# Another order of the on-chip buffers in a three-part transformer block

## The reference

```python
def _swiglu(x, w_in, w_out):
    a, b = jnp.split(x @ w_in, 2, axis=-1)
    return (jax.nn.silu(a) * b) @ w_out

for layer in range(DEPTH):
    h = h + 0.5 * _swiglu(_rmsnorm(h, ffn1_norm[layer]), ffn1_w_in[layer], ffn1_w_out[layer])
    ...
    h = h + 0.5 * _swiglu(_rmsnorm(h, ffn2_norm[layer]), ffn2_w_in[layer], ffn2_w_out[layer])
```

## Time and profile before

| what | value |
|---|---|
| time of the profiled run | 2951.99 us |
| its span, first to last instruction | 2950.2 us |
| median of three runs | 2957.29 us |
| TensorE matmul busy | 2768.1 us, 94% |
| GpSimd busy | 1653.9 us, 56% |
| VectorE busy | 1369.8 us, 46% |
| ScalarE busy | 694.1 us, 24% |
| q1, the queue of the kernel's own DMAs | 234.21 MB, 25.7% of 16 DMA engines |
| mean granted clock of TensorE | 0.972 |

### The profile page before, as it was taken

One profiled execution on the slowest core, in us unless ns is written; L12 is line 12 of the kernel. 1 busy time (PEld: TensorE's weight loads), 2 busy tenths in 40 slices (PEclk: granted clock), 3 DMA queues, 4 the chain that ended last, 5 costly groups with the idle time before them and its releaser, 6 DMA issues. The chain is left out here.

```text
span 2950.2 us, 36065 instructions
## 1 busy us (share of the span) xinstructions
PE 2768.1 (94%) x13132; PEld 2200.9 (75%) x13132; DVE 1369.8 (46%) x1623; ACT 694.1 (24%) x1168; POOL 1653.9 (56%) x966
## 2 busy tenths in 40 slices
PE   7999989766799999997899999999999999999999
PEld 5777768543678888875688888878888866788887
DVE  8878842145453143115654143754144466543142
ACT  3444320233210011026421011121011166321010
POOL 4666746300456566650266566666666678666565
PEclk9999999877899999999999999999999989999999
DMA  4222223100223232320133232333233200133232
GB/s 168 93 93 97 88 79 91 52 0 0 72 79 114 78 103 89 96 83 1 35 94 110 82 100 94 100 120 107 86 99 96 71 7 2 37 99 114 78 96 89
DMA packets 62023, 235.59 MB, mean 80 GB/s; under 512 B 6880, under 2 KB 7008, under 8 KB 61792
## 3 DMA queue, kind: packets, MB, share of 16 engines
q1 hardware_dynamic: 61920, 234.21, 25.7%
HBM read 232.08 MB, written 2.10 MB: 79 GB/s over the span
## 5 line engine op out<-in xcount | busy, mean ns | idle before, releaser
L314 POOL TENSOR_TENSOR w_lo<-ring,w_hi 128x1024 fp32r<-128x1024 f32 (+2 forms) x396 | 1026.7, 2593 | 57.8 <-issue 2.6
L312 POOL CAST w_hi<-ring 128x1024 fp32r<-128x1024 f32 (+2 forms) x396 | 454.0, 1146 | 1040.2 <-PE ps L332 801.5
L330 PE MATMUL ps<-hi,w_hi 128*128 128x512 f32 x2064 | 811.4, 393 | 12.4 <-DVE lo L1381 4.6
L332 PE MATMUL ps<-hi,w_lo 128*128 128x512 f32 x2064 | 805.4, 390 | 0.0
L331 PE MATMUL ps<-lo,w_hi 128*128 128x512 f32 x2064 | 805.3, 390 | 0.0
L330 PEld LDWEIGHTS ps<-hi,w_hi 128*128 128x128 f32 x2064 | 388.7, 188 | 99.6 <-DVE lo L1381 6.5
L331 PEld LDWEIGHTS ps<-lo,w_hi 128*128 128x128 f32 x2064 | 388.6, 188 | 82.3 <-issue 2.6
L332 PEld LDWEIGHTS ps<-hi,w_lo 128*128 128x128 f32 x2064 | 388.6, 188 | 81.8
L330 PE MATMUL ps<-hid_hi,w_hi 128*128 128x512 f32 x704 | 274.4, 390 | 0.0
L331 PE MATMUL ps<-hid_lo,w_hi 128*128 128x512 f32 x704 | 274.0, 389 | 0.0
L332 PE MATMUL ps<-hid_hi,w_lo 128*128 128x512 f32 x704 | 273.9, 389 | 0.0
(11 more groups left out here) (307 smaller groups left out, 3441.4 us busy)
## 6 DMA issues: line engine op xcount, KB each, us to landing
ring<-in_ffn_in SPq DMA_DIRECT2D x176, 512.0 KB, 3.6
ring<-in_even_in SPq DMA_DIRECT2D x48, 512.0 KB, 4.4
ring<-in_ffn_out SPq DMA_DIRECT2D x32, 768.0 KB, 4.2
ring<-in_ffn_out SPq DMA_DIRECT2D x32, 640.0 KB, 3.8
ring<-in_even_out SPq DMA_DIRECT2D x16, 512.0 KB, 3.6
ring<-in_odd_v SPq DMA_DIRECT2D x8, 512.0 KB, 3.6
ring<-in_odd_qk SPq DMA_DIRECT2D x8, 512.0 KB, 3.6
ring<-in_odd_r SPq DMA_DIRECT2D x8, 512.0 KB, 3.6
```

Source lines behind the costliest of these rows:

```text
L312: nc.gpsimd.tensor_copy(w_hi[:, j % 2, 0:cols], ring[:, j, 0:cols])
L314: nc.gpsimd.tensor_tensor(w_lo[:, j % 2, 0:cols], ring[:, j, 0:cols], w_hi[:, j % 2, 0:cols].bitcast(F32), ALU.subtract).then_inc(sem["w_r ...
L330: nc.tensor.matmul(bank, w_hi[:, j % 2, w], x_hi[:, k, :], start=(start and k == 0), stop=False)
L332: mm = nc.tensor.matmul(bank, w_lo[:, j % 2, w], x_hi[:, k, :], start=False, stop=(stop and k == kt - 1))
```

## The change

The ten pieces of SBUF are laid down in another order. Sizes, names, instructions and their order on each queue stay as they are.

```diff
-        for name, cols in (("consts", (N_CONSTS + 7) // 8 * 8), ("small", 16), ("masks", 2 * P), ("res", DT * T),
-                           ("hi", DT * T), ("ring", RING * SLOT), ("root", T), ("rinv", T), ("acc", T), ("arena", ARENA)):
+        for name, cols in (("res", DT * T), ("hi", DT * T), ("ring", RING * SLOT), ("consts", (N_CONSTS + 7) // 8 * 8),
+                           ("root", T), ("rinv", T), ("acc", T), ("small", 16), ("masks", 2 * P), ("arena", ARENA)):
             put(name, cols)
```

## The result

The changed kernel takes 2991.33 us, the median of four runs (2990.14 to 3000.12), against 2956.15 us for four runs of the kernel before (2951.99 to 2961.56). The ratio is 1.0121, with a 95% interval of 1.0106 to 1.0138. The prediction was 2955 us, with a range of 2945 to 2968; both missed it. The profiled run took 2993.0 us, with a span of 2991.2 us.

A forecast was written before the change was run, and what follows sets the result against it. The prediction took TensorE, busy 94% of the span, as the bound. All terms were 0, so 2951.99 us for the profiled run plus 0; toward the three-run median of 2957.29 it said 2955 us, range 2945 to 2968.

The forecast's parts named there:

- Distance costs nothing: 0 us for the 8,304 matmuls of these two operand sets.: TensorE matmuls streaming `hi` or `hid_hi`: how far apart operands lie does not matter, since both showed 226.7 ns; 0 us.
- The 64-byte remainder: TensorE matmuls streaming `hi`, whose start goes from remainder 32 to 0 by 64 bytes: 0 us, bounded by 58 either way.
- +58 us: Upper bound on TensorE's loss if remainder 32 was the good case: 13.4 ns for each of 4,320 `hi` matmuls.
- the −58 side: Rival, faster through TensorE: `hi` at a multiple of 64 loses its excess per column, giving 2894 us; chance 0.05.
- the slower side: Outcome more than 0.3% slower, chance 0.09: through GpSimd's slots (0.06) or through TensorE's granted clock (0.03).
- VectorE: Durations at L1407, L245 and L1622 do not depend on start addresses: 0 us, at most 1 us at L245.
- GpSimd: Cast and subtraction per `ring` slot, covered by 1.86 us of idle time: 0 us, bounded by 6.5 us either way.
- the rival: GpSimd's subtraction slows from unlike remainders of `ring` and `w_hi`: 2965 us at 20% more per slot; chance 0.06.
- DMA: Landings before the first matmul at 10.80 us and first-layer weights: 0 us, at most 1.1 us at the start.
- the rival through the clock: Shifted VectorE and GpSimd phases move dips of TensorE's clock; two more 10 us stretches give 2962 us; chance 0.03.
- a rule on addresses "that all operands of before met by chance": Closing sign that the prediction is wrong: some engine has such a rule; no size or chance given.

The follow-up runs named there:

- run 2: Kernel before with `hi` 32 bytes further and what follows it 64 (distance 224 between `hi` and `w_hi`, mod 256): 2997.38 us.
- run 3: Kernel before with all pieces moved 32 bytes further: 2954.61 us.
- run 5: Kernel before with only the split weights `w_hi` and `w_lo` 32 bytes further, no stream moved: 3023.65 us, beside 2952.89 for the kernel before.
- run 6: Kernel before with `hi` 64 bytes further and what follows 128, `res` staying (distance 192 from `hi` to `w_hi`, mod 256): 3008.13 us.
- run 4: Kernel before with `res` and `ring` put at multiples of 64 and `hi` at remainder 32 by 64 (distance 192 to `w_hi`, mod 256): 3006.18 us.
- run 7: Kernel before with `ring` and all behind it, weights included, 128 bytes further and `hi` staying (distance 128): 2974.66 us.
- run 10: Separate kernel, TensorE alone on zeros: matmul triples at 16 stream-to-weights distances, both streams or one moved, plus float32 and bfloat16 matmuls; 338.9 us in all.
- run 9: Changed kernel with `arena` 32 bytes further, so `hi` to weights is a multiple of 256: 2953.03 us against 2961.07 for the kernel before, ratio 0.998.
- run 8: Kernel before with `ring` alone 32 bytes further, the rest moved by 256 or 0: 2956.18 us.
- run 1: Changed kernel with `res` to `ring` 32 bytes further and what follows 64 (distance 0): 2957.21 us, beside 2951.69 for the kernel before.
- run 11: Separate kernel, TensorE alone, zeros as output: one stream at several distances to the weights, then pairs with streams and weights moved one by one; 183.23 us in all.

## Why the prediction was wrong

**"Distance costs nothing: 0 us for the 8,304 matmuls of these two operand sets."** This is the step that failed. The earlier trace rows do show `hi` and `hid_hi` 77 KB apart at the same 226.7 ns. But both are multiples of 256 bytes from the weights, so the rows compared one case with itself, and the 0 was carried over to a case that they did not hold. What counts is the distance to the weights that are read beside the stream, by its remainder mod 256 (runs 2, 3, 5, 6). The table of the change had the fact: `hi` moves by 27,872 bytes, 108 x 256 + 224, and `arena`, with the weights, by none. The prediction asked for unlike remainders of two operands on GpSimd, for `ring` and `w_hi`, and not on TensorE, for `hi` and `w_hi`.

**"The 64-byte remainder": 0, because a start touches only the first and last group of a row.** The reason was wrong twice. The remainder by 64 has no effect by itself (runs 3 and 4). And that a remainder touches little of a row doesn't make it free: averaged over a triple, each spacing grew by 2 to 8 ns in runs 2 and 4 to 7. Where in a row this time is lost is open, since no run had another number of columns. The term was mis-sized: 0 taken, 35.8 us measured. Its own upper bound, +58 us, held the result, though by other matmuls than it counted: 13.4 ns for two matmuls in three, where all three lost 5.2 ns each and `token_product` lost time too. But it was left out of the range; only the −58 side became a rival, and the slower side had GpSimd and the clock as its causes. A range from 2945 to 3010 would have followed from the bounds as they stood.

The Trainium skill's lines of 16 bytes ("SBUF — State Buffer", section "Door 1: The DMA port swizzle") made the remainder harmless and so supported 0. The runs disagree with that use of it: distances of 16, 32 and 64 bytes, all multiples of 16, cost 1 to 3% of a triple (run 10).

**The rest of the sum** held. VectorE: L1622 at 692 ns as before, 0 taken. One of its lines did grow, the subtraction at L245, from 106.5 to 127.8 us over its 64 runs, against 1 us for an effect of its start. That has no price here: the waits of TensorE for it did not grow (11.0 us before and 10.5 after at L347), and run 9 has 132.4 us at that line with the time of before. It went from 97 to 148 us between the runs of this case, and why is not shown. GpSimd: 0 taken; 1.05 and 2.41 us in place of 1.04 and 2.39, covered by 1.99 us of idle time, and run 8 with its 2440 ns excludes the rival. DMA: the first matmul is at 10.81 us, where it was at 10.80, and the queue's share is 25.4%. The waits are those of before: 31.5 us at L670, and 9.0 us at L330 in place of 9.3. The clock: the time at the lower clock, summed over the span, grew from 167 to 188 us, but runs 1 and 9 had 184 and 178 us with the time of before, so the rival through the clock is not the cause of the 35 us. What came true was named only in the last sentence of the prediction, a rule on addresses "that all operands of before met by chance", and got no price.

## What to carry to other kernels

Two equal rows show that an address doesn't matter, but only if their addresses differ in the way that the change does: work out the remainders of both against the other operand, by 64, 128, 256 and 512, before using them. With F32R operands, keep each stream a multiple of 256 bytes, or better 512, from the weights that TensorE reads beside it; a pad of 8 columns gave back the 1.2% here (run 9). And where a bound for an unseen case is worked out, both of its ends belong in the range, whatever the reason for the value taken.

## What the runs showed of the hardware

- F32R matmuls of 512 columns run 226.7 ns apart when stream and weights are a multiple of 256 bytes apart, and on average 229 to 238 ns over a triple with a stream at another distance (run 10; 226.7 also at 240, where every stream had that distance). At the upper clock, 2.4 GHz, these are 544 and 549 to 572 cycles. No distance tried averaged below 226.7 over a triple, so none gave back the 13.4 ns over 213.3.
- Two matmuls of three out of step cost as much as all three: 698.8 ns (`hi` alone at 224, run 2) against 700.0 (all streams at 224, run 5).
- One distance can have two rhythms: the changed kernel had stretches with triples of 700 ns and others of 698 and 688 ns in turn, and changed between them only at a break. What sets the rhythm is not shown.
- Plain float32 (429 ns a record) and bfloat16 (215.8 ns) showed no such effect at any distance tried.
- The Trainium skill, "SBUF — State Buffer", section "Who interferes with whom", gives TensorE two independent read ports, one for the moving operand and one for the weight load, and says that TensorE never waits on anyone. No run here contradicts the last point: the price is there with no other engine at work (run 10). But for F32R the two operands are not independent in time: the address of the stream against that of the weights changes the spacing from 226.7 to 233 ns (runs 10 and 11). That the two ports are what meets is not shown.
